# Stick-breaking sums: one fp32 product replaced by two fp32r products on split operands

## The reference

```python
z = jnp.einsum('bqhd,bkhd->bhqk', q[:, q0:kl], k[:, :kl]).astype(jnp.float32) * scale
mask = s_pos < t_pos
log_stay = jnp.where(mask, jax.nn.log_sigmoid(-z), 0.0)
between = lax.cumsum(log_stay, axis=3, reverse=True) - log_stay
a = jnp.where(mask, jnp.exp(jax.nn.log_sigmoid(z) + between), 0.0)
outs.append(jnp.einsum('bhqk,bkhd->bqhd', a.astype(v.dtype), v[:, :kl]))
```

## Time and profile before

| what | value |
|---|---|
| median of 3 runs | 1455.23 us (1453.64 to 1455.31) |
| the profiled execution | 1451.91 us, span 1450.1 us |
| mean granted TensorE clock | 0.993 of full |
| busy: TensorE | 1410.1 us, 97% |
| busy: VectorE | 1128.7 us, 78% |
| busy: ScalarE | 932.1 us, 64% |
| busy: GpSimd | 47.9 us, 3% |

### The profile page before, as it was taken

The page is one execution under the profiler, slowest core; times in us unless marked ns, Lnnn a source line. Parts: engine busy times, 40 slices in busy tenths (PEclk is TensorE's granted clock), DMA queues, the critical chain, the costliest instruction groups (busy, mean ns, idle before and its releaser), DMA issues.

```text
span 1450.1 us, 19281 instructions
## 1 busy us (share of the span) xinstructions
PE 1410.1 (97%) x7417; PEld 1200.2 (83%) x7417; DVE 1128.7 (78%) x843; ACT 932.1 (64%) x742; POOL 47.9 (3%) x58
## 2 busy tenths in 40 slices
PE   7999999999999999999999999999999999999996
PEld 6877899988977788888888888888888888888885
DVE  5674554545674799988898898888888889889897
ACT  4454443434554577777777777777777777777775
POOL 0011000000011002000000000000000000000200
PEclk9999999999999999999999999999999999999999
DMA  8741796555542599999999999999999999999992
GB/s 307 258 146 58 282 354 222 183 194 162 172 146 62 199 356 395 393 398 394 389 376 392 384 365 384 394 357 397 383 370 387 382 380 373 385 397 357 396 395 104
DMA packets 190547, 450.61 MB, mean 311 GB/s; under 512 B 7529, under 2 KB 10638, under 8 KB 190494
## 3 DMA queue, kind: packets, MB, share of 16 engines
q1 hardware_dynamic: 188270, 442.43, 83.3%
q0 software_dynamic: 1936, 6.86, 1.3%
q10 hardware_dynamic: 288, 0.59, 0.1%
HBM read 431.49 MB, written 18.36 MB: 310 GB/s over the span
## 4 chain that ended last, share of the span: by engine, by line
PE 92%; DVE 3%; DMA 2%; ACT 1%; POOL 1%; SPq 1%; issue 0%; DVEq 0%
PE ps L511 86%; PE ps L852 2%; DMA raw<-in_w_in 1%; PE ps L608 1%; DVE hn L1178 1%; POOL hn L476 1%; DMA hn<-bias_scratch 1%; PE ps L632 0%; PE ps L810 0%; PE ps L655 0%; DVE aT_lo L1186 0%; DMA bias_scratch<-vrow 0%; DVE w_lo L350 0%; PE ps L821 0%; PE ps L597 0%
## 5 line engine op out<-in xcount | busy, mean ns | idle before, releaser
L350 DVE TENSOR_TENSOR w_lo<-raw,w_hi 128x2048 fp32r<-128x2048 f32 x401 | 914.9, 2291 | 208.9 <-ACT w_hi L345 208.1
L345 ACT ACTIVATE w_hi<-raw 128x2048 fp32r<-128x2048 f32 x401 | 768.0, 1917 | 314.4 <-PE ps L511 304.3
L511 PE MATMUL ps<-w_hi,xe_hi 128*128 128x512 f32 x896 | 244.7, 395 | 0.0
L511 PE MATMUL ps<-w_hi,xe_lo 128*128 128x512 f32 x896 | 240.0, 390 | 0.0
L511 PE MATMUL ps<-w_lo,xe_hi 128*128 128x512 f32 x896 | 239.9, 389 | 0.0
L511 PEld LDWEIGHTS ps<-w_hi,xe_lo 128*128 128x128 f32 x896 | 168.2, 188 | 35.9
L511 PEld LDWEIGHTS ps<-w_lo,xe_hi 128*128 128x128 f32 x896 | 168.2, 188 | 35.5
L511 PEld LDWEIGHTS ps<-w_hi,xe_hi 128*128 128x128 f32 x896 | 164.6, 188 | 31.6
L511 PE MATMUL ps<-w_hi,he_hi 128*128 128x512 f32 x448 | 120.6, 391 | 0.0
L511 PE MATMUL ps<-w_lo,he_hi 128*128 128x512 f32 x448 | 119.9, 389 | 0.0
L511 PE MATMUL ps<-w_hi,he_lo 128*128 128x512 f32 x448 | 119.8, 389 | 0.0
(11 more groups left out here) (220 smaller groups left out, 956.9 us busy)
## 6 DMA issues: line engine op xcount, KB each, us to landing
raw<-in_expert_w_gate SPq DMA_DIRECT2D x112, 1024.0 KB, 7.8
raw<-in_expert_w_up SPq DMA_DIRECT2D x112, 1024.0 KB, 8.0
raw<-in_expert_w_down SPq DMA_DIRECT2D x112, 1024.0 KB, 7.8
raw<-in_w_in SPq DMA_DIRECT2D x24, 1024.0 KB, 7.8
raw<-in_dense_w_gate SPq DMA_DIRECT2D x11, 1024.0 KB, 6.6
raw<-in_dense_w_up SPq DMA_DIRECT2D x11, 1024.0 KB, 8.2
raw<-in_dense_w_down SPq DMA_DIRECT2D x11, 1024.0 KB, 4.8
raw<-in_w_out SPq DMA_DIRECT2D x8, 1024.0 KB, 5.1
```

Source lines behind the costliest of these rows:

```text
L345: nc.scalar.activation(w_hi[:, n % SPL, :], raw[:, n % RAW, :], ACT.Copy).then_inc(hi_ready, 1)
L350: nc.vector.tensor_tensor(w_lo[:, n % SPL, :], raw[:, n % RAW, :], w_hi[:, n % SPL, :].bitcast(F32), ALU.subtract).then_inc(lo_ready, 1)
L511: return pe.matmul(o, stationary, moving, start=start, stop=stop, skip_group_check=True)
```

## The change

Every pair's masked softplus `spl` is split into `stays_hi` (fp32r, ScalarE) and `stays_lo` (fp32r, VectorE), and `add_stays` multiplies each half with an fp32r copy of the two constant matrices, `tri_r`. `stays_hi` lies on the memory of `ab`, and `stays_lo` on the memory of `spl`. So `minus_abs(g)` for g of 2 and 3 also waits until the sums of pair g - 2 are done.

```diff
-            ab = sp_("ab", [P, 2, 2, ZW])
+            with ExitStack() as logs:
+                ab = sb("ab", [P, 2, 2, ZW], F32, logs)
+            stays_hi = sp_("stays_hi", [P, 2, 2, ZW], F32R)
...
-            spl = sp_("spl", [P, 2, 2, ZW])
+            with ExitStack() as stays:
+                spl = sb("spl", [P, 2, 2, ZW], F32, stays)
+            stays_lo = sp_("stays_lo", [P, 2, 2, ZW], F32R)
...
+            tri_r = sp_("tri_r", [P, 2, P], F32R)
...
                 def add_stays(g):
-                    pe.wait_ge(spm_done, PAIRS * l + g + 1)
-                    for m in range(2):
-                        bank = ps[:, (2, 4)[g % 2] + m, :]
-                        pe.matmul(bank[:, 0:ZW], neg_tri, spl[:, g % 2, m, :], start=False, stop=False, skip_group_check=True)
-                        last = pe.matmul(bank[:, P:S], neg_one, spl[:, g % 2, m, S:ZW], start=False, stop=True,
-                                         skip_group_check=True)
+                    if g == 0:
+                        pe.wait_ge(tri_ready, l + 1)
+                    for half, ready in ((stays_hi, stay_hi), (stays_lo, stay_lo)):
+                        pe.wait_ge(ready, PAIRS * l + g + 1)
+                        for m in range(2):
+                            bank = ps[:, (2, 4)[g % 2] + m, :]
+                            part = half[:, g % 2, m, :]
+                            pe.matmul(bank[:, 0:ZW], tri_r[:, 0, :], part, start=False, stop=False, skip_group_check=True)
+                            last = pe.matmul(bank[:, P:S], tri_r[:, 1, :], part[:, S:ZW], start=False, stop=(half is stays_lo),
+                                             skip_group_check=True)
                     last.then_inc(tri_done, 1)
...
+                def high_stays(g):
+                    act.wait_ge(spm_done, PAIRS * l + g + 1)
+                    copy(stays_hi[:, g % 2], spl[:, g % 2]).then_inc(stay_hi, 1)
...
                 stay_logs(0)
                 split_hi(act, n0 + 11)
+                high_stays(0)
...
                 split_hi(act, n0 + 13)
+                high_stays(1)
+                high_stays(2)
...
                 turned(3 * l + 1, (2, 3), 6, 0)
+                high_stays(3)
                 split_hi(act, n0 + 14)
...
+                    if g >= 2:
+                        dve.wait_ge(tri_done, PAIRS * l + g - 1)
...
+                def low_stays(g):
+                    dve.wait_ge(stay_hi, PAIRS * l + g + 1)
+                    V.tensor_tensor(stays_lo[:, g % 2], spl[:, g % 2], stays_hi[:, g % 2].bitcast(F32), ALU.subtract).then_inc(stay_lo, 1)
...
                 split_lo(dve, n0 + 10)
+                V.tensor_copy(tri_r[:].rearrange("p a k -> p (a k)"), cst[:, C_NTRI:C_NTRI + 2 * P]).then_inc(tri_ready, 1)
                 minus_abs(0)
...
                 softplus(0)
                 split_lo(dve, n0 + 11)
+                low_stays(0)
...
                 split_lo(dve, n0 + 13)
+                low_stays(1)
+                low_stays(2)
...
                 turned(3 * l + 1, (2, 3), 6, 0)
+                low_stays(3)
                 split_lo(dve, n0 + 14)
```

More of the change, by code:

```diff
@@ L265, in build @@
             sem(n) for n in ("z_done", "absz_done", "ln_done", "sp_done", "spm_done", "tri_done", "a_done", "am_done", "pv_done"))
+        tri_ready, stay_hi, stay_lo = sem("tri_ready"), sem("stay_hi"), sem("stay_lo")
         z0_done, zd0_done, v_df_saved = sem("z0_done"), sem("zd0_done"), sem("v_df_saved")
```

## The result

| | median us | runs | lowest to highest |
|---|---|---|---|
| before | 1453.64 | 7 | 1450.38 to 1455.31 |
| after | 1468.34 | 7 | 1461.60 to 1474.73 |

The ratio is 1.0104, with a 95% interval of 1.0076 to 1.0131: slower by 1.0%, 14.7 us. I forecast +6.5 us, 1461.7, with a range up to 1466.0. The sign was right and the size less than half of it.

A forecast was written before the change was run, and what follows sets the result against it. TensorE, busy 97% of the span, bounds the kernel. Shorter products less new waits add about 3.3 us a layer, 6.5 in all after rounding: 1455.2 + 6.5 = 1461.7 us, range 1457.5 to 1466.

The forecast's parts named there:

- TensorE's own work: Sums of each pair: two fp32r halves cost 1.15 us instead of 1.74, saving 4.7 us over 8 pairs if nothing waits.
- sign of being wrong: Stated test at the sums: wrong if a product of 384 or 128 columns costs more than 0.2 us.
- 0.11 us floor by a weight load: 128-column fp32r products in the sums were taken to cost at least 0.11 us, set by loading weights.
- The new passes: Added work: high half on ScalarE 0.87 us, low half on VectorE 0.97, copy of the constants 0.30.
- The waits: Per layer: +1.95 (pair 0), +1.74 (pair 1), -0.59 (pair 2), +0.84 (copy of v), -0.59 (pair 3), about 3.3 us.
- Pair 0: First pair's sums: TensorE waits for both halves and ends at 88.99 instead of 87.04 us, +1.95 us.
- the shift at the first product with v: After the copy of v, delayed by the later row norm, TensorE's total shift is 3.94 us.
- The idle before the low products: Pairs 0 and 1 of each layer: TensorE idles 1.87 us until VectorE delivers the low half.
- Pair 3: Last pair's sums: both halves ready in time, so -0.59 us; its mask and values covered by 2.4 us.
- (3): Rival: SBUF passes much quicker, 1458.6 us, or 1457.2 without the old clock stretch; chances 0.05 slower, 0.08 within 0.2%.
- rival (1): New TensorE idling costs the clock, about 1.4 us per fall; one or two falls give 1463.1 to 1464.5; chance 0.13.
- Neither theory: Experiments' theories for lost clock: TensorE doing little, by idling or narrow products, or the fp32r products by themselves.

The follow-up runs named there:

- e8: Changed kernel with the new passes placed in the ScalarE and VectorE queues where their inputs come, same work; 1452.72 us, ratio 1.0002 to before.
- e3: Changed kernel without the low pass on VectorE: the high half is multiplied twice, the low half left out of the sum; 1453.62 us, ratio 1.0001 to before.
- e4: Kernel before with softplus written as fp32r and one fp32r product, no low half, no new pass but the constants' copy; 1457.48 us, ratio 1.0012.
- e6: e4 with 8 filler products on TensorE before the first product with v; 1447.77 us, ratio 0.9964 to before.
- e5: Changed kernel with unread filler products between the halves of pairs 0 and 1 and before the first product with v; 1459.47 us, ratio 1.0046 to before.
- e9: Changed kernel with filler products only before the first product with v (5 of them); 1460.35 us, ratio 1.0054 to before.
- e10: Changed kernel with filler products only between the high and low products of pairs 0 and 1 (6 and 7); 1460.37 us, ratio 1.0051 to before.
- e11: e8 with filler products ahead of the second half of w_out, 6 before the turned rows and 7 behind; 1449.94 us, ratio 0.9982 to before.
- e12: Kernel before with the same filler products as e11 ahead of the second half of w_out; 1450.85 us, ratio 0.9987 to before.
- e7: Kernel before, fp32 products kept, with the copy of v on ScalarE made twice; 1455.79 us, ratio 1.0023 to before.

## Why the prediction was right and wrong

**TensorE's own work: right in the sum.** A half was to cost 0.58 us. The chain of after has 0.44 + 0.06 + 0.23 + 0.06 for the low half of pair 0, which starts after a wait, and e8 and e3 have 0.58 (twice 0.23 + 0.06) for a half that does not. The single terms were off: 384 columns take 0.23 us and 128 columns 0.06, where I had 0.177 and 0.111, so the two errors cancel and the good sum is in part luck. 0.23 is also over the 0.2 us that I had named as a sign of being wrong. The 0.11 us floor by a weight load does not hold for them. The gain itself is real: e4 has 8.0 us less rest, and its two runs that lost no more than before are 5 to 7 us faster, where a walk had 4.6.

**The new passes: right.** 0.85 us on ScalarE, 0.95 on VectorE and 0.29 for the constants, against 0.87, 0.97 and 0.30.

**The waits: right in place, about right in sum.** Pair 0 cost +1.6 us (forecast +1.95), the shift at the first product with v was 3.2 (3.9), a layer without the clock 2.65 (3.3). For both layers the profile gives 5.3 us and I had 6.5; the runs give +4.4 by the medians of the rest and up to 6.9 at about equal loss. The idle before the low products was 1.43 and 1.67 us, not 1.87. e8 shows that the place in the queues is the cause. Pair 3 was covered as forecast: the chain of after goes through its sums without a wait. The lower end of my range stands at 1457.5 where (3) with the clock adds up to 1457.2; nothing hangs on it.

**The clock: the step that failed.** The sum of 6.5 us has no term for the clock. It stands only in rival (1), where I wrote that each fall costs about 1.4 us, that there would be one or two, and gave it 0.13. The mechanism was named, but left at nothing in the sum, and its size was read from one stretch of 3.3 us in before. In the profile of after there are falls at two places in each layer, of 3.4 and 10 us, plus one more behind the turned rows of layer 1. There the clock makes 15.6 of the 21.0 us (1.6 of them at the bias near 45.7 us, ahead of the change); over the runs the loss is +10.3 us, of which 7 to 10 are time. One long fall alone made 4.75 us. The long fall has no counterpart in the rows of before: it lies over products of 64 columns and short sums, and lasts until the twelve 512-column products of a half piece have run. I also looked only at the idle pieces that the new passes make. Shorter products make one by themselves where the next input comes no sooner: in e4 no wait for a half was added, TensorE idled 1.56 us before the values, and the loss is the same 20.4 us. Fillers in that piece bring 8.8 us of it back (e6).

**What stays open.** Work in the gaps holds the clock (e5, e6, e9, e10 to within about 4 us of the loss of before, e11, e12), and better order does too (e8). Neither theory is enough alone: e7 idles 1.30 us with fp32 products and mostly holds, e3 idles 1.08 us with fp32r products and holds in its profile, after idles 0.88 us and falls. How much of it is the idle piece, how much the pieces before it and how much chance is not settled. Chance has a part: after alone lost 13.1 to 30.9 us over its seven runs, and at the bias near 45.7 us TensorE idled 2.29 us in the profile of before and 2.20 in that of after, ahead of the same four products, which took 1.99 us in the one and 3.68 in the other. No run has the fp32 product with the idle piece of e4 (1.56 us), so the part of the shorter products beside that piece is not measured.

## What to carry to other kernels

A shorter product on TensorE is only a gain if its operands are there. A pass that makes them belongs at the place in each queue where its input comes, not behind the next long pass; here that order was worth about 1% with the same work. Before pricing a wait or a shorter product on a TensorE-bound path, ask what the clock will do behind it. Compute (1 - granted clock) x span for each run, but check in windows that TensorE was busy where the clock was low, since a low clock over idle time costs nothing. Try filling gaps of a microsecond with products that nothing reads, and see whether the time falls and not only the loss. The length of one fall in one profile is not the price of the next: here the same kernel had falls of 3.4 and of 10 us.

## What the runs showed of the hardware

- fp32r products of 128 columns next to one of 384, with another stationary matrix each, took 0.06 us, and fp32 passes of 64 or 128 columns 0.11 us. So 0.11 us is not a floor for fp32r.
- The falls behind the sums of pair 0 lasted about 3.4 us (after, e9), those ahead of the second half of w_out 3.4 us in before and after and 6.8 us in layer 0 of e8 and e6, and those in the values about 10 us (after, e4, e10), where 64-column fp32 products and sums came first.
- The loss to the clock varied within one kernel over its runs, 5.8 to 16.0 us for before and 13.1 to 30.9 for after, while the rest varied by 5 to 7 us.
